# Where sixteen modulation blocks are multiplied: inside the recurrent scan instead of in the readout and the delta merge

## The chip, the cores and the metric

The kernel runs on one core of a Trainium2 chip. The metric is the device time of one execution in microseconds (us), the median of several runs. TensorE multiplies, VectorE (DVE) and ScalarE (ACT) do elementwise work, GpSimd (POOL) a part of the masks, SyncE (SP) issues most DMAs. All data is float32; a large product is computed from pairs of rounded high and low parts.

## The reference, cut to what matters

Three residual layers over 256 tokens of width 1024 (the first two also carry 256 context tokens): a layer with window attention and an mLSTM, an RWKV-7 layer, and a layer with a gated delta rule, an SSD mixer and 32 experts. Each layer is modulated by its condition:

```python
sh_a, sc_a, gt_a, sh_m, sc_m, gt_m = adaln(c, ada_w[layer], ada_b[layer])   # silu(c) @ w + b, split in six
h = rms_norm(x) * (1.0 + sc_a) + sh_a
...
s = s * wt[:, :, None, :] + sa[..., None] * bt[:, :, None, :] + vt[..., None] * kt[:, :, None, :]   # RWKV-7 state
```

`ada_w` of one layer is 1024 x 6144. The kernel cuts it into 12 blocks of 1024 x 512 (2 MB each), and each block is multiplied with the two columns of the condition (latent and context). These products depend on nothing but the condition, so they may stand anywhere ahead of the first use of their values.

## The kernel before

The program is a row of phases. A phase declares its tiles and semaphores, and writes one instruction list for each engine; between two phases all engines meet.

**The ring.** Large weights stream through one ring of three 2 MB slots (class Ring). `plan_ada`, `plan_cols` and `plan_rows` write the order of all its blocks at the start. A phase that takes n blocks calls `ring.issue(sync, n)`, which lets SP issue the loads of these n blocks and of the three after them, each as two DMAs of 1 MB, as soon as the block that held the slot is marked done (`gemm_done`). So up to three blocks of a later phase lie ready when it starts.

**A modulation block** (class Modulate). Eight products of a 128 x 2 weight (the condition) with 128 x 512 of the block; four of them write partitions 0, 32, 64 and 96 of one PSUM bank side by side, and the other four add to them (L746). ACT copies the bank to `mod_row` (L727). Four matmuls with `mod_row` as the weight and the 2-column table `fold` turn the row into columns and add the four parts (L732). At the end DVE adds the bias and writes `g.mods` (L758). The bank is cleared at first, since only two of each 32 partitions are written (L721). In the trace each float32 matmul leaves two records, so a block has 16 matmul records in L746 and 8 in L732.

**The recurrent scan** (`rw_chunks`) does 8 tile steps: four context or latent tiles of 128 tokens forward, then four backward; steps 2, 3, 6 and 7 are latent ones and compute an output too (`read`). A step holds 16 heads, two chunks of 64 tokens and two lanes, all as 64 x 64 matmuls of about 15 to 29 ns each. In order on TensorE: `products`, `first_level`, then levels k = 1 to 5 of a triangular inverse (`level_t`, `level_yx`) with pieces of the next tile's preparation between them (`logits`, `totals` at k = 2, `cumulate` at k = 3), then `solve`, `carry` (products PT on L2217, then G on L2225 and L2229), `read` if latent (L2240 to L2251), `chunk` (L2265, L2278) and `turn_in` of the next tile (L2128). The turn-in waits for ACT's copy of G (L2384) and for DVE's scaled tiles of the next step (L2473 to L2478, semaphore `s_til`).

SP loads k, kk, r of step i once step i-1 has been scaled (`s_til`), and v of step i once G of step i-2 is done.

**The readout** (`rw_readout`) follows the scan: group norm of the output on DVE (L2643 to L2651), then for each of two token tiles seven elementwise steps and the gate (L2656 to L2666), then transposes on TensorE (L2606) and copies on ACT (L2625). TensorE multiplies eight modulation blocks around this. **The delta merge** (`gd_merge`) is built alike (L3486 to L3505 on DVE, transposes L3445, copies L3469) with another eight blocks. `gemm_feat` ("rwout", and "about" in the first layer) and `gemm_rows` ("mixout") are the products after them.

`keep_busy(g, dst, n)` issues n matmuls of 128x128 with 128x256 whose result nobody reads (L482), at the start of many phases.

## Time and profile before

| | us |
|---|---|
| median of 3 runs | 3275.87 (3272.88 to 3277.51) |
| profiled execution, its own time | 3276.72 |
| its span (first to last instruction) | 3274.6 |
| scan, first `products` to the end | 1028.6 to 1529.0 |
| readout | 1529.0 to 1576.3 |
| delta merge | 2121.5 to 2166.4 |

The times in the trace are microseconds from the start of the span. Busy shares of the whole span: TensorE 90%, DVE 41%, ACT 29%, POOL 10%. The shares say little of one stage: the last third of the span is the experts, which stream 400 MB of weights. The stages of the change are in the middle.

### The profile page before, as it was taken

To read this page: it belongs to the slowest core of one execution; us is meant where nothing else is said; L and a number is where in the kernel's file an instruction comes from. 1 tells how busy PE (TensorE), PEld (TensorE's weight loads), DVE (VectorE), ACT (ScalarE), POOL (GpSimd) and SP (SyncE) were. 2 spreads that over 40 slices of the span, in tenths; PEclk is the share of its full clock that TensorE was granted. 3 is DMA by queue.
4 is the path that set the end of the run, shared out by engine and by line. 5 is a ranking of instruction groups with operands and counts; after the bars stand their busy time and mean duration, and the time that the engine had idled before them with its cause. 6 is when DMAs were issued, how large, how long until landed. Compare 5 with 4: busy or idle time off the path is not lost. (4 is left out here: it accounts for less than half of the span.)

```text
span 3274.6 us, 79289 instructions
## 1 busy us (share of the span) xinstructions
PE 2935.4 (90%) x35148; PEld 1967.2 (60%) x35148; DVE 1331.3 (41%) x2021; ACT 948.7 (29%) x1646; POOL 314.5 (10%) x253
## 2 busy tenths in 40 slices
PE   7988899999997788787899988798999998998996
PEld 5865577888575666665799877675333333333332
DVE  3355544333763654555455676464110110110112
ACT  3124433222343333432444563432100100100101
POOL 0021200000321122122000002310000000000001
PEclk9999899999998999999899998988999999999997
DMA  7262412222153100003555432088999999999996
GB/s 267 78 243 78 171 52 103 99 82 103 64 195 114 55 23 23 29 29 109 211 180 181 158 129 81 9 293 306 374 421 421 421 422 421 421 422 421 421 422 265
DMA packets 195063, 681.03 MB, mean 208 GB/s; under 512 B 25616, under 2 KB 40464, under 8 KB 145312
## 3 DMA queue, kind: packets, MB, share of 16 engines
q1 hardware_dynamic: 175328, 651.93, 51.2%
q10 hardware_dynamic: 18336, 21.21, 1.8%
q8 instruction: 203, 3.33, 0.4%
q0 software_dynamic: 1152, 4.19, 0.4%
q14 instruction: 44, 0.36, 0.0%
HBM read 651.86 MB, written 25.43 MB: 207 GB/s over the span
## 5 line engine op out<-in xcount | busy, mean ns | idle before, releaser
L4006 PE MATMUL experts_psum_gu<-ring,experts_x 128*32 128x512 f32 x3840 | 431.4, 597 | 34.6 <-DMA ring<-in_w_gu 34.6
L4128 DVE TENSOR_SCALAR experts_gate<-experts_psum_gu 128x768 f32<-128x768 f32 (+1 forms) x32 | 26.4, 824 | 850.2 <-PE experts_psum_gu L4006 850.2
L4006 PEld LDWEIGHTS experts_psum_gu<-ring,experts_x 128*32 128x32 f32 x3840 | 111.9, 110 | 336.2 <-issue 241.5
L4035 PE MATMUL experts_psum_down<-down_weights,experts_hiddenT 128*32 128x256 f32 x4096 | 231.2, 381 | 15.6 <-DMA down_weights<-in_w_down 12.7
L4035 PEld LDWEIGHTS experts_psum_down<-down_weights,experts_hiddenT 128*32 128x32 f32 x4096 | 127.5, 110 | 128.1 <-DMA down_weights<-in_w_down 32.9
L4072 ACT ACTIVATE experts_sigmoid<-experts_gate 128x768 f32<-128x768 f32 (+1 forms) x32 | 23.6, 737 | 584.9 <-DVE experts_gate L4128 584.9
L991 PE MATMUL mlp_psum_bank<-mlp_x_high,mlp_w_high 128*128 128x512 f32 (+1 forms) x512 | 175.5, 343 | 7.1 <-DVE ring_rounded L315 4.5
L315 DVE TENSOR_TENSOR ring_rounded<-ring,mlp_w_high 128x1024 fp32r<-128x1024 f32 x128 | 156.8, 1225 | 44.4 <-ACT mlp_w_high L310 44.4
L991 PE MATMUL mlp_psum_bank<-xT_rounded,mlp_w_high 128*128 128x512 f32 (+1 forms) x512 | 173.5, 339 | 0.0
L1001 PE MATMUL mlp_psum_bank<-mlp_hidden_high,mlp_w_high 128*128 128x512 f32 (+1 forms) x512 | 172.2, 336 | 1.2 <-ACT mlp_relu L937 1.2
L991 PE MATMUL mlp_psum_bank<-mlp_x_high,ring_rounded 128*128 128x512 f32 (+1 forms) x512 | 173.1, 338 | 0.0
L1001 PE MATMUL mlp_psum_bank<-mlp_hidden_high,ring_rounded 128*128 128x512 f32 (+1 forms) x512 | 172.0, 336 | 0.0
L1001 PE MATMUL mlp_psum_bank<-mlp_hidden_rounded,mlp_w_high 128*128 128x512 f32 (+1 forms) x512 | 172.0, 336 | 0.0
L4006 PE MATMUL experts_psum_gu<-xT,experts_x 128*32 128x512 f32 x1280 | 146.0, 594 | 14.7 <-DMA xT<-in_w_gu 14.7
L2080 POOL TENSOR_TENSOR rwkv_Lo<-rwkv_L,rw_shared 128x512 f32<-128x512 f32 x80 | 101.9, 1285 | 430.6 <-DVE rwkv_L L2512 321.6
L310 ACT CAST mlp_w_high<-ring 128x1024 fp32r<-128x1024 f32 x128 | 133.5, 1043 | 0.0
L991 PEld LDWEIGHTS mlp_psum_bank<-mlp_x_high,mlp_w_high 128*128 128x128 f32 x512 | 97.4, 190 | 20.4 <-issue 5.9
L4006 PEld LDWEIGHTS experts_psum_gu<-xT,experts_x 128*32 128x32 f32 x1280 | 36.7, 110 | 120.6 <-issue 82.4
L4168 POOL DMA_INDIRECT slot_tokens<-moe_y,y_index x8 | 10.2, 1271 | 1018.4 <-POOLq L3949 1016.3
L991 PEld LDWEIGHTS mlp_psum_bank<-mlp_x_high,ring_rounded 128*128 128x128 f32 x512 | 97.8, 191 | 12.2
L1001 PEld LDWEIGHTS mlp_psum_bank<-mlp_hidden_high,mlp_w_high 128*128 128x128 f32 x512 | 97.2, 190 | 11.8 <-ACT mlp_relu L937 1.8
L991 PEld LDWEIGHTS mlp_psum_bank<-xT_rounded,mlp_w_high 128*128 128x128 f32 x512 | 97.0, 189 | 10.5
(793 smaller groups left out, 6052.5 us busy)
## 6 DMA issues: line engine op xcount, KB each, us to landing
ring<-in_w_gu SPq DMA_DIRECT2D x192, 1024.0 KB, 25.9
down_weights<-in_w_down SPq DMA_DIRECT2D x96, 1024.0 KB, 27.2
ring<-in_ada_w SPq DMA_DIRECT2D x72, 1024.0 KB, 10.8
ring<-in_mlp_w SPq DMA_DIRECT2D x64, 1024.0 KB, 7.0
xT<-in_w_gu SPq DMA_DIRECT2D x64, 1024.0 KB, 26.0
ring<-in_w_in SPq DMA_DIRECT2D x24, 1024.0 KB, 6.4
spare_unit<-in_w_down SPq DMA_DIRECT2D x16, 1024.0 KB, 27.1
x<-in_w_down SPq DMA_DIRECT2D x16, 1024.0 KB, 27.3
```

What stands on the lines that cost most here:

```text
L310: self.g.nc.scalar.copy(h, w).then_inc(self.s_high, 1)
L315: self.g.nc.vector.tensor_tensor(low, w, h.bitcast(F32), ALU.subtract).then_inc(self.s_low, 1)
L991: mm = nc.tensor.matmul(banks[:, f % 8, 0:n_tok], w[:, kt, :], x, start=(kt + k == 0), stop=(kt == KT - 1 and k == 2))
L1001: mm = nc.tensor.matmul(banks[:, b, 0:n_tok], w[:, 0, cols], h, start=(f + k == 0), stop=(f == FT - 1 and k == 2))
L2080: v.tensor_tensor(Lo[l][:, :, :], L[l][:, :, :], rep(small(C2_LVL + HALF_LEVELS * d + k), M8), ALU.mult).then_inc(s_lo[l], 1)
L4006: mm = nc.tensor.matmul(pg[32 * j:32 * j + 32, gr, :, :], x, strip(w, j), start=False, stop=(u == U - 1))
L4035: mm = nc.tensor.matmul(pd[32 * c:32 * c + 32, gr, :], hidT[:, a, gr, GROUP * v:GROUP * v + GROUP], w[:, a, C * c:C * c + C], start=(v == ...
L4072: nc.scalar.activation(sg[:, 0:groups, :], gt[:, 0:groups, :], ACT.Sigmoid, scale=SWI_ALPHA).then_inc(s_sg, 1)
L4128: v.tensor_scalar(G, pg[:, 0:groups, 0, :], SWI_LIMIT, None, ALU.min).then_inc(s_gt, 1)
L4168: nc.gpsimd.indirect_dma_start(out=yl[:, n, :], out_offset=None, in_=y_dram[:, :], in_offset=bass.IndirectOffsetOnAxis(ap=yidx[:, t, k:k + ...
```

## The change

1. `rw_chunks` gets a `ScanModulate` with two blocks a tile step, 16 in all: 4 for the RWKV layer's last part and all 12 of the third layer. Products of a step's two blocks go into bank 0 of each lane: those of step 0 after `cumulate(0)` and ahead of the first turn-in, those of step i+1 into the `carry` of step i, between PT and G. ACT copies both rows ahead of its copy of G. The folds of step i stand at k = 2 of step i, ahead of `totals(i + 1)`; ACT keeps their result (two copies of 128x8). TensorE waits for the row copies at the end of `carry`, and for the kept columns ahead of `cumulate`. SP issues the ring's loads behind the v load of each step.
2. The readout has no blocks; it adds the bias of all 16 (`ModulateBias.add`) ahead of its `fetch.wait`. The bias loads are issued behind the others. The square moves from DVE (1 of 1024 a tile) to ACT. `keep_busy` of 6 at the start, of 8 between the two tiles' transposes.
3. The delta merge has no blocks, no `keep_busy` of 4 at the start, and one of 8 between the two tiles' transposes.
4. `keep_busy` at the start goes from `gemm_feat` (5), `mlp` (2 and 4), `ab_merge` (4) and `gemm_rows` (5).

```diff
@@ class ScanModulate (new)
+    def products(self, pe, n, dst):
+        wv = self.ring.take(pe)
+        for kt in range(KT):
+            j = 32 * (kt % 4)
+            if kt == KT // 2:
+                self.ring.wait(pe, self.ring.used - 1, 1)
+            mm = self.g.nc.tensor.matmul(dst[j:j + 2, :], self.g.silu[:, self.dst[n][2] // 2, kt, :], wv[:, kt, :],
+                                         start=(kt < 4), stop=(kt >= 4))
+        self.ring.mark(mm)
+    def copy(self, act, n, src):
+        act.wait_ge(self.ring.gemm_done, self.done0 + n + 1)
+        if n >= self.each:
+            act.wait_ge(self.s_fold, n - self.each + 1)
+        self.g.nc.scalar.copy(self.row[:, n % self.each, :], src).then_inc(self.s_row, 1)
+    def fold(self, pe, n, dst):
+        pe.wait_ge(self.s_row, n + 1)
+        for f in range(4):
+            mm = self.g.nc.tensor.matmul(dst[:, 2 * f:2 * f + 2], self.row[:, n % self.each, f * P:(f + 1) * P], self.g.fold[:, :],
+                                         start=True, stop=True)
+        mm.then_inc(self.s_fold, 1)
+    def keep(self, act, n, src):
+        act.wait_ge(self.s_fold, self.each * (n // self.each + 1))
+        mods, first, _ = self.dst[n]
+        self.g.nc.scalar.copy(mods[:, first:first + 4, :], src.rearrange("p (a b) -> p a b", b=2)).then_inc(self.s_kept, 1)
...
@@ rw_chunks
+        sm = ScanModulate(g, ph, modulate, 2)
+        mod_at = lambda e: banks[e][:, 0, :]
+        fold_at = lambda e: banks[0][:, 3, 16 + 8 * e:24 + 8 * e]
@@ SP, behind the v load of each step, and once at the end
+                    g.ring.issue(sync, sm.each * i)
+                g.ring.issue(sync, sm.each * N)
@@ TensorE, totals(i)
+                    if i:
+                        folds(i - 1)
@@ TensorE, carry(i), between PT and G
+                    if i + 1 < N:
+                        modulate_step(i + 1)
...
+                    if i + 1 < N:
+                        pe.wait_ge(sm.s_row, sm.each * (i + 2))
@@ TensorE, before the loop
                 cumulate(0)
+                pe.wait_ge(s_zero, sm.each)
+                modulate_step(0)
                 take(s_til)
...
@@ rw_readout, TensorE
-                keep_busy(g, ps[:, 0, 0:256], 4)
-                m.step(pe, 0)
-                m.step(pe, 1)
+                keep_busy(g, idle[:, 0:256], 6)
                 gates.wait(pe)
...
-                for k in range(2, m.n - 1):
-                    m.step(pe, k)
                 turned(0)
-                m.step(pe, m.n - 1)
+                keep_busy(g, idle[:, 0:256], 8)
                 turned(1)
@@ rw_readout, DVE
-                    ch.link(nc.vector.tensor_tensor(sq[:, :], yt, yt, ALU.mult))
...
+                m.add(dve)
                 fetch.wait(dve)
@@ gd_merge, TensorE
-                keep_busy(g, ps[:, 0, 0:256], 4)
-                for k in range(m.n - 1):
-                    m.step(pe, k)
                 turned(0)
-                m.step(pe, m.n - 1)
+                keep_busy(g, idle[:, 0:256], 8)
                 turned(1)
@@ gemm_feat and gemm_rows; ab_merge loses its 4, mlp its 2 and 4
-                keep_busy(g, banks[:, 0, 0:256], 5)
@@ the ring's plan
         plan_ada(1, 8, 4)
-        plan_ada(2, 0, 4)
+        plan_ada(2, 0, 12)
...
-        plan_ada(2, 4, 8)
```

## Rows read from the trace of the kernel before

**Rows 1.** Busy time by stage: us, busy (instructions) of five engines, granted clock, DMA share, GB/s

```profile
1028.60:1529.00 500.40, 398.78 (x14312) 335.07 (x14312) 263.42 (x334) 187.74 (x327) 124.56 (x96) 0.97 0.08 27
1143.60:1213.10 69.50, 56.22 (x2000) 47.54 (x2001) 39.27 (x48) 26.35 (x46) 18.46 (x14) 0.98 0.09 27
1529.00:1576.30 47.30, 42.70 (x232) 18.90 (x232) 26.88 (x31) 8.45 (x14) 0.00 (x0) 0.79 1.00 354
2121.50:2166.40 44.90, 39.03 (x232) 19.31 (x232) 26.58 (x27) 15.77 (x23) 0.00 (x0) 0.73 0.92 342
```

**Rows 2.** Timeline of the readout: start, us, engine, line, tiles, count [idle before <- releaser]

```profile
1530.11 1.16 DVE L2643 TENSOR_REDUCE rwread_stats<-rw_y 128x16 f32<-128x1024 f32 x1
...
1541.66 1.23 DVE L2656 TENSOR_TENSOR rw_y<-rw_y,rwread_stats 128x1024 f32<-128x1024 f32 x1 [0.30 <-DMA v_lat<-rw_v]
...
1549.02 1.05 PE L732 MATMUL rwread_psum_mod<-fold,rwread_mod_row 128*128 128x2 f32 x8
...
1550.00 1.90 PE L746 MATMUL rwread_psum_mod_row<-ring,silu 128*2 128x512 f32 x16
...
1556.10 1.29 DVE L2666 TENSOR_TENSOR readout<-rw_y,rwread_psum_gate 128x512 f32<-128x512 f32 x2
...
1574.19 1.07 PE L2606 MATMUL rwread_psum_gate<-const,readout 128*128 128x128 f32 x8
...
1576.40 3.89 PE L482 MATMUL rwout_psum_bank<-const 128*128 128x256 f32 x10 [1.14 <-PEq L2583]
```

**Rows 3.** Timeline of the delta merge

```profile
2121.65 3.27 PE L482 MATMUL gdmerge_psum_turned<-const 128*128 128x256 f32 x8 [2.65 <-PEq L156]
...
2145.88 1.22 DVE L3505 TENSOR_TENSOR mix<-ys,sn 128x1024 f32<-128x1024 f32 x1
...
2152.29 1.23 DVE L3505 TENSOR_TENSOR mix<-ys,sn 128x1024 f32<-128x1024 f32 x1
...
2156.01 3.65 PE L3445 MATMUL gdmerge_psum_turned<-const,mix 128*128 128x128 f32 x16
...
2163.25 1.95 PE L3445 MATMUL gdmerge_psum_turned<-const,mix 128*128 128x128 f32 x16
...
2166.44 2.40 PE L482 MATMUL mixout_psum_bank<-const 128*128 128x256 f32 x10 [1.24 <-PEq L3431]
```

**Rows 4.** DMA queues in scan step 2, 1143.6 to 1213.1: packets, MB, share

```profile
q8 instruction: 16, 0.26, 1.6%
```

**Rows 5.** TensorE's timeline in the carry and read of step 2

```profile
1190.37 1.16 PE L2217 MATMUL rwkv_psum_lane<-rwkv_B,rwkv_A 64*64 64x64 f32 x64
1191.33 1.03 PE L2225 MATMUL rwkv_psum_lane<-rwkv_L,rwkv_B 64*64 64x64 f32 x56
1193.95 0.34 PE L2225 MATMUL rwkv_psum_lane<-rwkv_L,rwkv_B 64*64 64x64 f32 x8 [1.59 <-issue]
...
1197.97 0.34 PE L2240 MATMUL rwkv_psum_lane<-rwkv_mat_BR,rwkv_A 64*64 64x64 f32 x8 [1.93 <-issue]
...
1203.36 0.45 PE L2251 MATMUL rwkv_psum_lane<-x,rwkv_mat_KR 64*64 64x64 f32 x8 [1.56 <-issue]
```

**Rows 6.** Timeline of the carry of step 0

```profile
1078.52 0.62 PE L2229 MATMUL rwkv_psum_lane<-x,rwkv_K 64*64 64x64 f32 x26 [1.64 <-issue]
...
1079.17 1.07 ACT L2384 COPY rwkv_T<-rwkv_psum_lane 128x512 f32<-128x512 f32 x2 [5.26 <-PE rwkv_psum_lane L2229]
...
1080.34 1.07 PE L2128 MATMUL rwkv_psum_lane<-const,rwkv_A 128*128 128x128 f32 x8 [0.31 <-ACT rwkv_T L2384]
```

**Rows 7.** TensorE's timeline at k = 2 of step 0, and ahead of the first turn-in

```profile
1047.32 1.95 PE L2110 MATMUL rwkv_psum_lane<-rw_shared,rwkv_A 128*128 128x2 f32 x16
1049.19 0.69 PE L2179 MATMUL rwkv_psum_lane<-rwkv_T,rwkv_X 64*64 64x64 f32 x32
...
1022.52 1.97 PE L2128 MATMUL rwkv_psum_lane<-const,rwkv_A 128*128 128x128 f32 x8 [5.11 <-DVEq L2480]
```

**Rows 8.** Busy time by stretch around k = 2 of step 0, and at the start of "about"

```profile
1050.40:1053.80 3.40, 3.04 (x118) 2.88 (x112) 0.69 (x1) 2.15 (x4) 0.90 (x1) 0.50 0.02 5
...
404.60:408.70 4.10, 4.10 (x11) 3.29 (x11) 2.98 (x4) 4.10 (x8) 0.00 (x0) 0.50 1.04 387
```

**Rows 9.** SP's timeline in step 2: the loads of k and kk, then of v

```profile
1197.49 0.32 SPq L2059 DMA_DIRECT2D rwkv_loaded<-rw_k  x1
1197.85 0.43 SPq L2059 DMA_DIRECT2D rwkv_loaded<-rw_kk  x1
1203.90 0.32 SPq L2067 DMA_DIRECT2D x<-rw_v  x1
```

More of the change, by code:

```diff
@@ L759, in add, with __init__ @@
                                            ALU.add).then_inc(self.s_end, 1)
+        dve.wait_ge(self.s_end, len(self.parts))
+class ScanModulate:
+    def __init__(self, g, ph, parts, each):
+        self.g, self.ring, self.each = g, g.ring, each
+        self.dst = [(g.mods[layer % 2], 4 * f, layer) for layer, first, n, _ in parts for f in range(first, first + n)]
+        self.row = ph.sb("mod_row", [P, each, 512])
+        self.s_row, self.s_fold, self.s_kept = ph.sem("mod_row"), ph.sem("mod_folded"), ph.sem("mod_kept")
+        self.done0 = self.ring.done
+    def products(self, pe, n, dst):
[22 more added lines that the diff above has]
+        self.g.nc.scalar.copy(mods[:, first:first + 4, :], src.rearrange("p (a b) -> p a b", b=2)).then_inc(self.s_kept, 1)
@@ new lines, with __init__, sync, add @@
+class ModulateBias:
+    def __init__(self, g, ph, parts):
+        self.g, self.parts = g, parts
+        self.bias = ph.sb("mod_bias", [P, 4 * sum(n for _, _, n, _ in parts)])
+        self.s_b, self.s_end = ph.sem("mod_bias"), ph.sem("mod_added")
+    def sync(self, sync):
+        o = 0
+        for _, first, n, bias in self.parts:
+            sync.dma_start(self.bias[:, o:o + 4 * n], bias[:, 4 * first:4 * (first + n)]).then_inc(self.s_b, 16)
+            o += 4 * n
+    def add(self, dve):
+        dve.wait_ge(self.s_b, 16 * len(self.parts))
+        o = 0
+        for layer, first, n, _ in self.parts:
+            dst = self.g.mods[layer % 2][:, 4 * first:4 * (first + n), :]
+            self.g.nc.vector.tensor_tensor(dst, dst, rep(self.bias[:, o:o + 4 * n], 2, 2), ALU.add).then_inc(self.s_end, 1)
+            o += 4 * n
@@ L1980, with rw_chunks @@
 DECAY = math.exp(-0.5)
[L1983 removed]
+def rw_chunks(g, scr, low_w, low_a, w2, a2, ctab, b16, pick, rows, y, coef, tables, s_stored, modulate):
     nc = g.nc
@@ L2091, in _, with modulate_step, folds @@
                 take = Take(pe)
+                def modulate_step(i):
+                    for e in range(sm.each):
+                        sm.products(pe, sm.each * i + e, mod_at(e))
+                def folds(i):
+                    for e in range(sm.each):
+                        sm.fold(pe, sm.each * i + e, fold_at(e))
                 def logits(i, which):
@@ L2292, in _ @@
                 for q in range(nq):
+                    if q == 1:
+                        pe.wait_ge(sm.s_row, sm.each)
                     if q >= 2:
@@ L2313, in _ @@
                             totals(i + 1)
+                        elif k == 2:
+                            folds(i)
+                        if k == 3:
+                            pe.wait_ge(sm.s_kept, sm.each * (i + 1))
                         if nxt and k == 3:
@@ L2395, in _ @@
                 exp_a(0)
+                for e in range(sm.each):
+                    sm.copy(act, e, mod_at(e))
                 turned(0, 0, 4 if lat(0) else 3)
@@ L2417, in _ @@
                                 exp_a(i + 1)
+                        if k == 2:
+                            for e in range(sm.each):
+                                sm.keep(act, sm.each * i + e, fold_at(e))
                         for l in range(2):
@@ L2426, in _ @@
                         copy(lanes(at[i % 2][:, :])[:, :, l, :], banks[l][:, 0, :], s_w[l], s_wc[l])
+                    if nxt:
+                        for e in range(sm.each):
+                            sm.copy(act, sm.each * (i + 1) + e, mod_at(e))
                     for c in range(2):
@@ L2494, in chain @@
                     v.tensor_tensor(new, new, rep(pc[i % 2][:, :, c], CH, 2), ALU.mult).then_inc(s_s, 1)
+                for e in range(sm.each):
+                    v.memset(mod_at(e), 0.0).then_inc(s_zero, 1)
                 mix_k(0)
@@ L2586, in _ @@
                 gates.issue(sync)
-                m.bias_in(sync)
                 fetch.issue(sync)
-                m.ring.issue(sync, m.n)
+                m.sync(sync)
             @block.tensor
             def _(pe):
-                keep_busy(g, ps[:, 0, 0:256], 4)
-                m.step(pe, 0)
-                m.step(pe, 1)
+                keep_busy(g, idle[:, 0:256], 6)
                 gates.wait(pe)
@@ L2617, in _ @@
             def _(act):
-                for k in range(2):
-                    m.copy(act, k)
+                for t in range(2):
+                    act.wait_ge(s_mid, t + 1)
+                    nc.scalar.activation(out[:, t, :], y[:, t, :], ACT.Square).then_inc(s_sq, 1)
                 act.wait_ge(s_var, 1)
@@ L2626, in turned @@
                                        ps[:, 2 * t + j, :].rearrange("p (a b) -> p a b", a=4)).then_inc(s_ev, 1)
-                for k in range(2, m.n - 1):
-                    m.copy(act, k)
-                turned(0)
-                m.copy(act, m.n - 1)
-                turned(1)
+                for t in range(2):
+                    turned(t)
                 act.wait_ge(s_ev, 4)
@@ L3417, in _, with gd_merge @@
                 dve.wait_ge(s_oc, 4)
-def gd_merge(g, p2, og, ys, rows, mix, mixT, fetch, modulate):
+def gd_merge(g, p2, og, ys, rows, mix, mixT, fetch):
     nc = g.nc
@@ L3429, in gd_merge @@
         ps = ph.ps("turned", [P, 4, 512])
-        m = Modulate(g, ph, modulate)
+        idle = ph.ps("idle", [P, 512])
         with nc.Block() as block:
@@ L3461, in _ @@
                             .then_inc(s_sz, 1)
-                for k in range(4):
-                    m.copy(act, k)
                 act.wait_ge(s_ms, 1)
@@ L3470, in turned @@
                                        ps[:, j, :].rearrange("p (a b) -> p a b", a=4)).then_inc(s_ev, 1)
-                for k in range(4, m.n - 1):
-                    m.copy(act, k)
-                turned(0)
-                m.copy(act, m.n - 1)
-                turned(1)
+                for t in range(2):
+                    turned(t)
                 act.wait_ge(s_ev, 8)
@@ L3568, in products @@
                     return mm
-                keep_busy(g, banks[:, 0, 0:256], 5)
                 for k in range(parts):
@@ L4367, in layer1 @@
             rw_chunks(g, scr, low_w, low_a, w2, a2, ctab, b16, pick, {"ka": ka[:, :], "rk": rk[:, :]}, y, coef, tables,
-                      [(s, len(range(i, n_stores, 3))) for i, s in enumerate(s_stored)])
+                      [(s, len(range(i, n_stores, 3))) for i, s in enumerate(s_stored)], modulate)
         both.close()
```

27 lines of the change are left out of this document (12 added, 15 removed).

## The prediction

> **What bounds the kernel now.** I read the page first, then the windows by stage [rows 1]. TensorE is 90% busy over the whole span, but the stages of the change differ. In the scan it works 398.8 of 500.4 us at a granted clock of 0.97, and the DMA engines are nearly idle (share 0.08, 27 GB/s). In the readout and the merge it looks just as busy, but DVE's two token tiles set the end, and the DMA engines are full (1.00 and 0.92; 354 and 342 GB/s). The reader is to see that the change moves TensorE work from stages where something else bounds to one where TensorE leads, and 32 MB of transfers from full engines to idle ones.
>
> Next the timelines. In the readout [rows 2] DVE starts at 1530.11, reaches the value term at 1541.66 with 0.30 us idle (for v_lat), and is done at 1556.10 + 1.29 = 1557.4. But the second tile is turned at 1574.19, since all blocks but one stand ahead of it. The merge [rows 3] has DVE's tiles done at 2147.1 and 2153.5, the turns at 2156.01 and 2163.25.
>
> The scan needs a second look. In the carry of a latent step [rows 5] 64x64 matmuls run back to back: from 1190.37 to 1192.36 (1191.33 + 1.03) are 120 records in 1.99 us, then TensorE stands 1.59 us for nothing but "issue"; from 1193.95 on it works again, and stands 1.93 us ahead of 1197.97; another stall, of 1.56 us, ends 5.4 us later. The queues of that step [rows 4] show 16 instruction transfers, 0.26 MB, so 16 KB each; the step holds 2000 records [rows 1], 125 to a transfer. The spacing of the stalls and the 16 KB agree: I read them as TensorE running ahead of its own instruction stream. A stretch of short matmuls uses 125 records in about 2 us, and a transfer with what surrounds it supplies them in some 3.5 to 4 (1193.95 to 1197.97 is 4.02). The third stall lies behind the loads of k and kk [rows 9]: with them the interval was 5.39 us, 1.4 longer, which I take for contention.
>
> **The change part by part**, against the profiled execution: 3276.72 us (the median of the runs, 3275.87, is 0.85 below it).
>
> *A, readout.* DVE's chain stays: the square (about 1.2 us a tile, as the other 128x1024 operations) goes to ACT, but a semaphore's trip each way and two bias additions come in, so I leave its end at 1557.4. The second turn and the copy took 1576.40 - 1574.19 = 2.2 us [rows 2]; with 0.3 for the handover the output product starts at 1559.9 in place of 1576.4: **-16.5** (-17.5 to -15). What is late next is DVE itself.
>
> *B, merge.* Tile 0 can turn at 2147.3, at half clock 3.65 us [rows 3]; eight `keep_busy` at half clock, another 4, reach 2155.0. That is behind tile 1's end (2153.5), so the filler itself may hold the turn; then 1.95 and the copy, 3.2 together (2163.25 to 2166.44). 2158.2 in place of 2166.4: **-8.2** (-9.5 to -7).
>
> *C, products in seven carries.* A block took 1.90 us for 16 records [rows 2], two 3.8, seven times 26.6. Against it: 32 records last as long as one transfer of instructions. The stream gets one transfer ahead, and the stall in G (1.59 in step 2 [rows 5], 1.64 in step 0 [rows 6]) goes, in latent steps a part of the next too. I take 2.5 us back a step, so 1.3 stays: **+9** (6.5, where only the 32 records count, a quarter of a transfer of 3.7 us a step, to 26.6). ACT's two row copies (0.6 us each, as its 128x512 copies are 1.07 for two [rows 6]) run beside G, whose first 56 records alone take 1.03 [rows 5], about half of it, so TensorE's wait at the end of carry costs nothing; were G's cover gone, it would be 1.2. The turn-in waited 0.31 for ACT's copy of G anyway, so a late copy would show there directly.
>
> *D, folds at k = 2.* 16 records with a 128x128 weight and two columns; `totals` is the same form, 16 in 1.95 us [rows 7]. Seven times 13.6, and a last one under no `totals`. The level waits partly for DVE's and ACT's copies, so I take 1.2 of 1.95, and 0.7 for the last: **+9** (3.8, as 16 records are an eighth of a transfer, to 15.6). Queued behind them are `totals` and the next level's products, for which ACT's and DVE's copies wait.
>
> *E, instruction transfers beside the ring's.* Each step now loads 4.19 MB; at 354 GB/s [rows 1] that is 11.8 us of full engines, behind v, three or four instruction transfers long, so some 25 in all. The only measure is the 1.4 us of [rows 5, 9], beside lighter traffic. Not all are met in short-matmul stretches. I take 0.3 each: **+8** (0 to 20).
>
> *F, clock.* After the 16 two-column matmuls of `totals` the clock stood at 0.50 for 3.4 us (1050.4 to 1053.8) [rows 8], though the scan holds 0.97. Folds double that low stretch at k = 2; seven times 0.35: **+2.5** (0 to 7).
>
> *G, the first tile.* TensorE idled 5.11 us ahead of the first turn-in [rows 7]; 3.8 us of products fit into it, if the three blocks lie ready, and may find it a higher clock: **-1** (-1.7 to +2).
>
> *H, fillers.* `keep_busy` of 5 took 2.40 us at full and 3.89 at half clock [rows 2, 3]. Five phases lose theirs. Where weights are late anyway this is nothing ("about" starts at 0.50 with the DMA engines at 387 GB/s [rows 8]); else it saves 1 to 2 us and gives it back as slower first products. I sum it to **+0.5** (-3 to +4).
>
> Nothing else moves: the ring keeps its order and the experts are shifted as a whole.
>
> **Sum.** -16.5 - 8.2 = -24.7; 9 + 9 + 8 + 2.5 - 1 + 0.5 = +28.0; together +3.3, 3276.7 + 3.3 = 3280.0. Against the median that is +0.13%. Some 0.2% (6.5 us) is what a measurement tells from no change, so it counts as the same.
>
> That TensorE waits for its instructions can be set against the Trainium skill, page "Runtime: NRT & Kernel Launch", section "Instruction fetch mechanics": instructions are refilled in 16 KiB blocks while the present ones execute, and crossing a boundary is "mostly hidden". The 16 KB agree with the row, "hidden" does not (1.6 to 1.9 us of "issue"). By that rule term C would be its full 26.6 and E nothing; it is the first rival. On E, "DMA: Bandwidth & Descriptors", section "Issuing engines are not separate DMA queues", says that transfers started by different engines share the same 16 and interleave; no row here shows an instruction transfer beside full engines. Without it E would stay at its bounds above.
>
> **Rivals.**
> 1. *TensorE's time is all on the path.* The stalls don't come from the stream but return elsewhere, whatever is inserted. C 26.6, D 13.6, F 2.5, E 0, G -1, H 0.5: +42.2 - 24.7 = +17.5, 3294. For it: TensorE is busy 80% of the scan, and the stall follows about every 125 records, which an insertion only shifts. Against it: the added instructions carry few records for their time. 0.2.
> 2. *The loads starve TensorE.* C and D as forecast, but each of the 25 transfers under full engines costs 0.8, E 20, F 4, the rest as in the forecast: +16.8, 3293. For it: one load pair cost 1.4. Against: in step 2 it was on one interval only. 0.15.
> 3. *The scan is bound by the stream of instructions alone* (the other side). Added records cost their share of a transfer and nothing else: C 6.5, D 3.8, E and F 0, G -1.7, H 0.5: +9.1 - 24.7 = -15.6, 3261. It decides if contention is nothing and each stall gives back 2.9 us a step. For it: the stalls of [rows 5, 6] sum to 5.1 us in one carry and read. Against: TensorE also waits for DVE and ACT in the levels, and records are added. 0.27.
> 4. *The moved products do not shorten the merge and readout*, for DVE ends them later (bias, square by semaphore): 3 us each, +9. It is inside the next case's range; I give it no chance of its own.
>
> The forecast, within 6.5 us of before, has 0.38. So faster 0.27, same 0.38, slower 0.20 + 0.15 = 0.35. The range goes from just below the third rival's time to just past the first's: 3260 to 3298; what is left out is C at its full size together with E at its own (over 3300), and a stream-bound scan with merge and readout at their best.
>
> **What the changed profile would show.** The scan 27 to 30 us longer: the latent step of 69.5 us [rows 1] near 73. After PT and the products G without "issue" idle (C right) or with 1.6 us (rival 1). TensorE's "issue" idle larger in the 12 us behind each v load (E). Granted clock at k = 2 low for 5 us or more (F). Readout 31 us, its DVE rows unchanged and the second turn right behind them (A); merge 37 us, and if its second turn waits for nothing, `keep_busy` held it (B). Wrong it would be if stalls are no matter of the stream, if ring blocks come late (loads are issued a step ahead, so against 11.8 us there are some 60), or if lower clocks persist in the phases that lost their fillers.

## The result, and the profile after

The changed kernel takes 3300.52 us (median of 3, 3299.67 to 3308.14) against 3275.87: ratio of the timed runs 1.0089, 95% interval 1.0073 to 1.0106 (the two medians alone give 1.0075). A second set of runs of the same kernel gave 1.0091 (1.0072 to 1.0111). The forecast was 3280.0, "same", with a range of 3260 to 3298: the change makes the kernel 24.7 us slower where 4.1 were forecast, and lands 2.5 us outside the range. The profiled execution has a span of 3298.7 us, 24.1 more than before.

The windows by stage of the changed kernel, beside [rows 1] (scan from TensorE's first product of step 0 to its last matmul, and to the readout; readout; merge; step 2):

```profile
1026.00:1578.40 552.40, 457.08 (x14664) 372.68 (x14664) 262.01 (x332) 197.59 (x357) 123.66 (x96) 0.93 0.24 86
1026.00:1581.80 555.80, 457.08 (x14664) 372.69 (x14665) 263.29 (x334) 197.59 (x357) 123.66 (x96) 0.93 0.24 85
1581.80:1614.60 32.80, 19.50 (x60) 12.59 (x61) 25.25 (x31) 8.73 (x14) 0.00 (x0) 0.76 0.25 85
2157.60:2195.80 38.20, 8.54 (x49) 7.87 (x49) 27.23 (x28) 13.82 (x21) 0.00 (x0) 0.64 0.07 20
1149.60:1231.40 81.80, 66.80 (x2049) 54.34 (x2049) 39.01 (x48) 27.73 (x50) 18.48 (x14) 0.90 0.26 94
```

What to see: the readout and the merge are short, as meant. The scan is 555.8 us in place of 500.4, TensorE busy 457.1 in place of 398.8 (58.3 more), its granted clock 0.93 in place of 0.97; its idle time (552.4 - 457.1 = 95.3) is about what it was (497.0 - 398.8 = 98.2). Step 2 is the sharpest: 81.8 us in place of 69.5, clock 0.90 in place of 0.98.

The start of that step in TensorE's timeline, and below it the window from the first sign of half clock:

```profile
1149.55 3.43 PE L2217 MATMUL rwkv_psum_lane<-xT 64*64 64x64 f32 x203 [0.94 <-DVE xT L2580]
1157.11 1.76 PE L2217 MATMUL rwkv_psum_lane<-xT 64*64 64x64 f32 x53 [4.14 <-issue]
1159.63 1.87 PE L2230 MATMUL rwkv_psum_lane<-rw_shared,rwkv_T 64*64 64x64 f32 x30 [0.76 <-ACT rwkv_mat_KR L2471]
```

```profile
1155.20:1165.40 10.20, 7.53 (x134) 5.95 (x134) 2.29 (x4) 2.46 (x5) 2.49 (x2) 0.50 0.47 174
```

TensorE stands 4.14 us by "issue" (it waits for nothing that the profile shows) in the middle of the products, and from 1155.2 on come 10.2 us at a granted clock of 0.50, in which 30 records take 1.87 us. Before, the same products had this wait:

```profile
1148.54 1.40 PE L2142 MATMUL rwkv_psum_lane<-xT 64*64 64x64 f32 x80 [1.64 <-issue]
```

The queues of 1141 to 1160 show what ran beside the longer wait:

```profile
q1 hardware_dynamic: 2650, 6.22, 88.7%
q8 instruction: 4, 0.07, 1.4%
```

Four instruction transfers in 19 us, and the data transfers take 88.7% of the sixteen engines. Narrow windows of the same view tell when each instruction transfer began. In step 2 of before it was at 1142.4, 1146.0, 1149.7 and 1153.3, one every 3.7 us; here it was at 1148.5, 1154.8, 1159.9 and 1163.5. So the second came 6.3 us behind the first and the third 5.2 behind the second, and with the loads gone the interval is 3.6 again. One of these windows (1154.75 to 1155.00):

```profile
q1 hardware_dynamic: 44, 0.09, 97.2%
q8 instruction: 1, 0.02, 28.1%
```

A transfer itself is no longer than it was (28.1% of sixteen engines in 0.25 us are 1.1 us of one engine; the mean over the scan is 1.06 us before and 1.02 after): it begins late. And TensorE's waits follow these transfers. All 16 "issue" waits of over 1 us in the changed scan end 2.2 to 2.7 us after one began, and so do all 23 of the kernel before: the 4.14 us end at 1157.11, 2.4 behind 1154.8, the 1.64 us of before at 1148.54, 2.6 behind 1146.0. From the first products to the end of the scan no engine's wait ends with the landing of a load, in either trace, so late data are not the cause. The waits of TensorE by line, before and after, in the stretch of the scan (us in total, times, longest), the products' line and then the level's:

```profile
PE rwkv_psum_lane L2142 <- issue: 8.0, 7, 1.7
PE rwkv_psum_lane L2170 <- issue: 16.6, 44, 0.9
```

```profile
PE rwkv_psum_lane L2217 <- issue: 16.8, 7, 4.4
PE rwkv_psum_lane L2245 <- issue: 13.9, 41, 0.7
```

The carry of step 1, where the block products stand (L778):

```profile
1134.81 1.29 PE L2292 MATMUL rwkv_psum_lane<-rwkv_B,rwkv_A 64*64 64x64 f32 x64
1136.03 3.62 PE L778 MATMUL rwkv_psum_lane<-ring,silu 128*2 128x512 f32 x32
1139.57 1.16 PE L2302 MATMUL rwkv_psum_lane<-rwkv_L,rwkv_B 64*64 64x64 f32 x64
1140.56 1.11 PE L2306 MATMUL rwkv_psum_lane<-x,rwkv_K 64*64 64x64 f32 x64
```

No idle time stands in front of the two parts of G; the 1.6 us of [rows 5] and [rows 6] are gone. Over the whole scan, the two lines of G before (L2225, L2229) and all that is left of their waits after:

```profile
PE rwkv_psum_lane L2229 <- issue: 6.3, 4, 1.7
PE rwkv_psum_lane L2225 <- issue: 5.6, 4, 1.6
```

```profile
PE rwkv_psum_lane L2306 <- issue: 1.3, 1, 1.3
```

And k = 2 of step 2, with the folds (L791), and its window:

```profile
1176.63 1.95 PE L791 MATMUL rwkv_psum_lane<-fold,rwkv_mod_row 128*128 128x2 f32 x16
1178.44 2.99 PE L2185 MATMUL rwkv_psum_lane<-rw_shared,rwkv_A 128*128 128x2 f32 x16
1181.36 1.14 PE L2254 MATMUL rwkv_psum_lane<-rwkv_T,rwkv_X 64*64 64x64 f32 x32
```

```profile
1178.40:1185.90 7.50, 7.50 (x178) 7.30 (x177) 0.74 (x1) 2.16 (x7) 1.87 (x1) 0.54 0.01 2
```

The fold takes 1.95 us, `totals` behind it 2.99 in place of 1.95 [rows 7], and the clock is 0.54 in the mean of 7.5 us, so some 6.9 of them at half (worked out from the mean), where [rows 8] had 3.4.

The readout and the merge, as [rows 2] and [rows 3]:

```profile
1581.81 1.22 DVE L2734 TENSOR_REDUCE rwread_stats<-rw_y 128x16 f32<-128x1024 f32 x1 [2.06 <-PEq L156]
...
1593.29 0.36 DVE L820 TENSOR_TENSOR mod<-mod,rwread_mod_bias 128x32 f32<-128x32 f32 x2 [2.90 <-DMA rwread_mod_bias<-in_adab_col]
...
1608.12 1.28 DVE L2760 TENSOR_TENSOR readout<-rw_y,rwread_psum_gate 128x512 f32<-128x512 f32 x2
1609.52 1.09 PE L2702 MATMUL rwread_psum_gate<-const,readout 128*128 128x128 f32 x8 [1.38 <-DVEq L2762]
...
1611.74 0.20 ACT L365 ACTIVATE rwout_token_root<-const 128x4 f32<-128x4 f32 x1 [0.45 <-PEq L2682]
...
1614.62 0.55 PE L626 MATMUL rwout_psum_bank<-rwout_x_high,rwout_w_high 128*128 128x256 f32 x1 [4.00 <-DVE readoutT_rounded L341]
...
2157.63 1.28 ACT L3549 ACT_TABLE_LOAD   x1 [3.85 <-PEq L156]
...
2183.23 3.29 PE L3537 MATMUL gdmerge_psum_turned<-const,mix 128*128 128x128 f32 x16 [28.25 <-DVEq L3589]
...
2186.36 3.62 PE L482 MATMUL gdmerge_psum_idle<-const 128*128 128x256 f32 x16
...
2189.82 1.91 PE L3537 MATMUL gdmerge_psum_turned<-const,mix 128*128 128x128 f32 x16
...
2192.95 0.20 ACT L365 ACTIVATE mixout_token_root<-const 128x4 f32<-128x4 f32 x1 [0.44 <-PEq L3524]
```

DVE's work in the readout lasts from 1581.81 to 1609.4, 27.6 us, and took 27.3 before; a wait of 2.90 us for the bias load has taken the place of the squares that ACT does now. The second turn follows at once.

Where a phase ends is best read from ACT's first instruction of the next one, since TensorE's first was a filler before and is a product now, which waits (4.00 us above). The same places before:

```profile
1576.38 0.20 ACT L365 ACTIVATE rwout_token_root<-const 128x4 f32<-128x4 f32 x1 [0.45 <-PEq L2583]
...
2121.61 1.28 ACT L3460 ACT_TABLE_LOAD   x1 [3.83 <-PEq L156]
...
2166.41 0.20 ACT L365 ACTIVATE mixout_token_root<-const 128x4 f32<-128x4 f32 x1 [0.44 <-PEq L3431]
```

So the readout went from 47.4 to 29.9 us (-17.5), its second turn from 45.2 to 27.7 us behind its start, and the merge from 44.8 to 35.3 (-9.5).

From the first TensorE instruction of one phase to the next one's, in us, the two traces give for the whole kernel (with the reservation just made on the rows behind the readout and the merge):

| | before | after | difference |
|---|---|---|---|
| all ahead of the scan | 998.5 | 997.6 | -0.9 |
| scan (phase) | 530.5 | 584.3 | +53.8 |
| readout | 47.4 | 32.8 | -14.6 |
| output product, up to the delta rule | 466.2 | 464.6 | -1.6 |
| delta rule and merge | 123.9 | 116.5 | -7.4 |
| mixing product and router | 101.3 | 96.5 | -4.8 |
| experts and the end | 1006.9 | 1006.5 | -0.4 |

And the scan by steps, from one first product to the next (to the last matmul for step 7):

| step | 0 | 1 | 2 latent | 3 latent | 4 | 5 | 6 latent | 7 latent |
|---|---|---|---|---|---|---|---|---|
| before | 57.2 | 57.7 | 69.5 | 66.8 | 57.6 | 61.2 | 70.8 | 56.1 |
| after | 62.6 | 61.0 | 81.8 | 77.4 | 62.9 | 63.0 | 85.5 | 58.2 |

The four context steps grew by 15.8 us together, 3.9 each, which is about what the forecast gave every step (28.0 over seven). The latent steps 2, 3 and 6 grew by 37.6, 12.5 each.

### The profile page after: what moved, and what is told of

The parts are those of the page before. It is cut to its first block and busy times, and to the rows that moved or that the text cites. A ratio compares the mean times of both kernels' runs of the same rounds, so it can differ in the third digit from the quotient of the medians.

```text
span 3298.7 us, 79244 instructions
## 1 busy us (share of the span) xinstructions
PE 2928.9 (89%) x35114; PEld 1972.9 (60%) x35114; DVE 1321.2 (40%) x2018; ACT 950.9 (29%) x1664; POOL 313.6 (10%) x253
## 6 DMA issues: line engine op xcount, KB each, us to landing
down_weights<-in_w_down SPq DMA_DIRECT2D x96, 1024.0 KB, 27.7
ring<-in_ada_w SPq DMA_DIRECT2D x72, 1024.0 KB, 11.5
```

## The experiments

Theory 1: the ring's loads keep the DMA engines full, TensorE's instruction transfers come late, and the idle time and what follows it lower the clock; it says where the largest part of the growth comes from. Theory 2, the forecast's first rival: the added products and folds take the time themselves. Three kernels take one part of the change out of the scan each, a fourth restores the fillers.

**Without the loads.** `no_loads` takes the sixteen blocks out of the ring's plan; the products use the three blocks that lie there.

```diff
@@ ScanModulate.products
-        wv = self.ring.take(pe)
+        b = self.ring.used + n % 3
+        self.ring.wait(pe, b, 0)
+        self.ring.wait(pe, b, 1)
+        wv = self.ring.buf[:, b % SLOTS, :].rearrange("p (a b) -> p a b", a=8)
...
-        self.ring.mark(mm)
+        mm.then_inc(self.s_prod, 1)
@@ SP
-                    g.ring.issue(sync, sm.each * i)
-                g.ring.issue(sync, sm.each * N)
@@ the ring's plan
-        plan_ada(1, 8, 4)
-        plan_ada(2, 0, 12)
```

> The changed kernel without the sixteen blocks' loads in the scan: its products multiply whatever the three blocks hold that lie ready when the scan starts, so the modulation values are not the reference's; every product, copy and fold stays. Theory 1 (the loads fill the DMA engines, TensorE's instruction transfers come late in the latent steps' products, and the idle time lowers the clock): the latent steps of 81.8, 77.4 and 85.5 us go to about 73, 70 and 74, 25 to 28 us less in all, 3300 - 26 = 3274. Theory 2 (the added products and folds themselves take the time, wherever it shows): within 5 us of the changed kernel, 3296 to 3301.

Its total (ratio 1.0216, 1.0182 to 1.0250) says nothing, since the modulation values were arbitrary and the experts' phase took 1034 us in place of 973; the scan went from 584.3 to 562.3. `no_loads2` sets the values to zero in the readout:

> The kernel of no_loads once more, with the modulation values of the scan's sixteen blocks set to zero in the readout, so that the experts see ordinary numbers (in no_loads their phase alone took 1034 us in place of 973). By the scan of no_loads (562.3 us from its start to the readout, the changed kernel 584.3, the kernel before 530.5): 22 us less than the changed kernel, about 3279.

Measured: 3276.11 us, ratio 1.0010 (0.9995 to 1.0025), 0.8% under the changed kernel, 26 us. The step starts give 75.0, 70.3 and 73.0 us for steps 2, 3 and 6. That is theory 1's number, and theory 2 as a whole account fails. But products and folds are not free: this kernel, with some 26 us saved in the readout and the merge, is not faster than the one before. The products of step 2 there:

```profile
1144.21 3.43 PE L2217 MATMUL rwkv_psum_lane<-xT 64*64 64x64 f32 x200 [0.94 <-DVE xT L2580]
1149.31 1.04 PE L2217 MATMUL rwkv_psum_lane<-xT 64*64 64x64 f32 x56 [1.67 <-issue]
```

The same stall, at the same place in the instructions, is 1.67 us and not 4.14. The 1.67 that stay are about what the kernel before had there (1.64).

**The loads alone.** Here each block is waited for and marked done, and nothing is multiplied, copied or folded.

```diff
@@ ScanModulate.products
-        wv = self.ring.take(pe)
-        for kt in range(KT):
...
-        self.ring.mark(mm)
+        self.ring.take(pe)
+        self.ring.wait(pe, self.ring.used - 1, 1)
+        pe.sem_inc(self.ring.gemm_done, 1)
+        self.ring.done += 1
```

> The changed kernel with only the loads in the scan: the products, their copies, folds and kept columns are left out (modulation values are missing), TensorE waits for each block and marks it done at the same place. Theory 1: the latent steps keep some 8 to 10 us of their growth, all added TensorE work goes (about 3.5 us a step), the first products stall for 4 us of issue as in the changed kernel: 3300 - 26 = 3274. Theory 2: the loads cost nothing, the scan has its old 500 us: 3300 - 54 = 3247.

Measured: 3278.06 us, ratio 1.0026 (1.0013 to 1.0038). The scan's phase took 556.7, 26 us more than before, with not one matmul added to TensorE's work, and none of its waits in the scan ends with the landing of a block. Theory 1 again. What the changed kernel has above this one, 21 us by the ratios, is products and folds.

**Without the folds.**

```diff
@@ TensorE, totals
-                    if i:
-                        folds(i - 1)
@@ TensorE, levels
-                        elif k == 2:
-                            folds(i)
-                        if k == 3:
-                            pe.wait_ge(sm.s_kept, sm.each * (i + 1))
@@ ACT, level k = 2
-                            for e in range(sm.each):
-                                sm.keep(act, sm.each * i + e, fold_at(e))
```

> The changed kernel without the folds at k = 2 and ACT's kept columns (the modulation values are missing). By the prediction's terms D and F: 9 + 2.5 = 11.5 us less, 3289. If each fold stands in full and draws a longer stretch at half clock behind it: 7 x (1.95 + 1) and more, 20 us less, 3280. If folds are hidden: 4 us less, 3296.

Measured: 3289.37 us, ratio 1.0043 (1.0015 to 1.0071), 15 us under the changed kernel; its scan phase was 560.9, 23 under the changed kernel's and 16 under that of its second trace (`after_again`, below). The forecast was 11.5: the traces say more, the timed runs can't tell 15 from it, with some 11 us on either side. `fold_one` keeps every wait and copy, and drops three of four matmuls:

```diff
@@ ScanModulate.fold
-        for f in range(4):
+        for f in range(1):
@@ ScanModulate.keep
-        self.g.nc.scalar.copy(mods[:, first:first + 4, :], src.rearrange("p (a b) -> p a b", b=2)).then_inc(self.s_kept, 1)
+        self.g.nc.scalar.copy(mods[:, first:first + 4, :], rep(src[:, 0:2], 4)).then_inc(self.s_kept, 1)
```

> The changed kernel with one fold matmul for each block in place of four (its result is copied to all four places, so the modulation values are wrong): 4 records a step at k = 2 in place of 16, the same waits and copies. If the folds' own time and the low clock behind them make the 23 us that no_folds saves in the scan: 15 to 18 us of them go here, scan 567. If the waits around them (row copies, kept columns) make it: less than 6 us go, scan 580.

Measured: ratio 1.0050 (1.0035 to 1.0065), about 13 us under the changed kernel; its scan phase 572.9, 11 under. By the times nearly all that `no_folds` saved, by the trace half of it, or less against the second trace of the changed kernel (4 of 16). What the waits around the folds cost is not settled.

**Without the products.** Loads, row copies, folds and kept columns stay, TensorE's part is that of `loads_only`, and the values are set to zero.

> The changed kernel without the products of the blocks in the scan (TensorE waits for each block and marks it done; loads, row copies, folds and kept columns stay; the modulation values are set to zero in the readout). The prediction's term C says 9 us less than the changed kernel. The runs so far leave 4 to 8 us for it (loads alone 26 more than before in the scan, folds 23, all together 54). If the products stood in full: 25 us less, ratio 1.001.

> The changed kernel itself, beside no_products on the same chip, to see how far the scan's time moves between executions (the scans of no_loads and no_loads2, the same instructions, took 562.3 and 550.5 us from their start to the readout): scan 580 to 590, ratio 1.007 to 1.011.

Measured: `no_products` 1.0081 (1.0049 to 1.0113), `after_again` 1.0091 (1.0072 to 1.0111), scan phases 577.3 and 576.5. The products cost next to nothing: 3 us by the ratios, with an interval of some 12 on either side, none by this pair of traces. The scan of the changed kernel took 584.3 in one trace and 576.5 in the other, those of `no_loads` and `no_loads2`, equal in instructions, 562.3 and 550.5: a difference of under 12 us between two single traces of the scan is worth little.

TensorE in the scan, from its first product to its last matmul, one window for each kernel. In order: before; changed; `no_loads2`; `loads_only`; `no_folds`; `no_products`.

```profile
1028.70:1525.70 497.00, 398.76 (x14312) 335.02 (x14312) 262.13 (x332) 187.74 (x327) 124.56 (x96) 0.97 0.08 27
```

```profile
1020.70:1566.00 545.30, 456.80 (x14664) 373.02 (x14664) 262.47 (x332) 197.45 (x357) 123.50 (x96) 0.93 0.24 87
```

```profile
1022.80:1542.40 519.60, 444.03 (x14664) 362.03 (x14664) 262.32 (x332) 197.51 (x357) 123.45 (x96) 0.95 0.08 27
```

```profile
1024.40:1547.50 523.10, 412.15 (x14312) 346.50 (x14312) 262.30 (x332) 187.45 (x327) 125.44 (x96) 0.93 0.25 90
```

```profile
1022.20:1552.00 529.80, 434.10 (x14536) 348.74 (x14536) 263.83 (x332) 195.55 (x341) 123.61 (x96) 0.94 0.25 90
```

```profile
1025.10:1568.80 543.70, 439.85 (x14440) 376.42 (x14440) 263.56 (x332) 195.91 (x357) 123.47 (x96) 0.91 0.24 86
```

(The second is `after_again`.) These rows part waiting from working. The loads alone: the same 14312 records last 412.2 us in place of 398.8, 13.4 more, and the idle time is 111.0 in place of 98.2, 12.8 more; so half of their 26 us is instructions that come late, and half is the same work at a lower clock. The same loads beside products and folds, `no_loads2` to `after_again`, give the same again: 12.8 us more work and 12.9 more idle time. Products and folds without loads: 45.3 us more work and 22.6 us less idle time (75.6). Products beside the loads, `no_products` to `after_again`: 17 us more work, 15 us less idle time. Seven pairs of blocks at 3.62 us are 25.3, so the rest of the work became 8 us shorter, at a clock of 0.93 in place of 0.91. The give-back that the forecast counted on for the products is there.

**Where the loads stand.** If only the products of latent steps were hurt, the loads could be moved. `late` holds them to level 1, `spread` puts each 1 MB behind an event of its own.

```diff
@@ late, SP
+                    if i:
+                        sync.wait_ge(s_sw, 2 * (i + 1))
                     g.ring.issue(sync, sm.each * i)
@@ spread, SP
+                    if i:
+                        g.ring.issue(sync, sm.each * i, ((s_sw, 2 * (i + 1)), (s_tot, i + 1), (s_cum, 2 * (i + 1)), (s_ea, i + 1)))
+                    else:
+                        g.ring.issue(sync, 0)
@@ spread, Ring.issue, ahead of each of the two loads of a block
+            if gates:
+                sync.wait_ge(*gates.pop(0))
```

> The changed kernel with SP waiting for the w sigmoid of the next tile (at level 1) before the ring loads of a step, so that they run during levels 1 and 2 and not under the products. If only the products and the first level (back to back matmuls without other waits) suffer from late instructions: products of latent steps back to 6 to 7 us, scan 8 to 12 us shorter, 573. If instructions are late wherever the engines are full: the loss moves into the levels, scan within 4 us of 584.

> The changed kernel with each of the four 1 MB loads of a step behind an event of its own (level 1, totals at k = 2, cumulate at k = 3, the exponentials at k = 4). A single 1 MB keeps the DMA engines full for 3 us, shorter than one interval between instruction transfers: if a delay needs a long queue, most of the 22 us go, scan 565. If each byte loaded costs the same: scan 580 to 584.

Measured: `late` 3316.45 us, 1.0124 (1.0098 to 1.0150), scan phase 600.5; `spread` 3297.52, 1.0070 (1.0047 to 1.0092), 581.5. Neither brings the time back. In `late` the products are cured (6.6 and 6.2 us in steps 2 and 3 in place of 10.1 and 10.3), and from the first matmul of level 1 to `totals` it takes 14.0 to 14.8 us in place of about 10.2. TensorE's waits there, the line of `level_t`, and one place:

```profile
PE rwkv_psum_lane L2247 <- issue: 32.7, 44, 3.1
```

```profile
1177.50 0.41 PE L2247 MATMUL rwkv_psum_lane<-rwkv_Y,rwkv_Lo 64*64 64x64 f32 x10 [0.28 <-issue]
1180.79 0.91 PE L2247 MATMUL rwkv_psum_lane<-rwkv_Y,rwkv_Lo 64*64 64x64 f32 x22 [2.88 <-issue]
```

16.6 us of "issue" on that line before, 32.7 here, and the 2.88 us end 2.5 us after an instruction transfer began (at 1178.3, the one before it at 1167.0). The folds behind such a wait run at half clock too: 3.57 us in place of 1.95 in six of the eight steps. So late instructions hurt in each of the three placings tried, and more in the first levels than under the products; spreading the loads in time leaves their price about as it is.

**The fillers.** `fillers` puts the removed `keep_busy` back.

> The changed kernel with the removed keep_busy back at the start of gemm_feat (5), mlp (2 and 4), ab_merge (4) and gemm_rows (5). By the prediction's term H: 0.5 us less, 3300. By the traces of the two kernels, where the phases behind the moved blocks are 1.5 to 2.5 us shorter each without them: 6 to 8 us more, 3307.

Measured: 3298.32 us, ratio 1.0075 (1.0046 to 1.0105), against 1.0089 and 1.0091 without them. The difference can't be told from nothing, on either side. In its trace `ab_merge` up to the RWKV layer's projection is 4.7 us longer than in the changed kernel's, the output product with what follows it 2.1 shorter, and the mixing product 1.5 shorter. (The readout ends at 29.7 us by ACT, as without them.)

**A version for use.** The runs say: a load in the scan costs 26/32 = 0.8 us a MB, folds at k = 2 cost 2 us or more a step, products little, and the readout's second turn is worth most (17.5 us, the merge's 8 to 9.5). `scan2` multiplies just the two blocks ahead of the first turn-in in the scan, the readout keeps six and the merge eight; `scan4` takes two more in the carry of step 0.

```diff
@@ rw_chunks, M = 1 (scan2) or 2 (scan4)
-                    g.ring.issue(sync, sm.each * i)
-                g.ring.issue(sync, sm.each * N)
+                    g.ring.issue(sync, sm.each * min(i, M))
...
-                    if i:
+                    if 0 < i <= M:
                         folds(i - 1)
...
-                    if i + 1 < N:
+                    if i + 1 < M:
                         modulate_step(i + 1)
@@ rw_readout and gd_merge: as before the change, and the readout adds the bias of the scan's blocks
@@ the ring's plan
-        plan_ada(2, 0, 12)
+        plan_ada(2, 0, 4)
...
+        plan_ada(2, 4, 8)
```

> A version for use. Only the two blocks ahead of the first turn-in are multiplied in the scan (TensorE idles 5.1 us there); their folds stand at k = 2 of step 0; the readout keeps six blocks, in the old order around its turns, and the merge its eight; the phases' keep_busy stay removed. By the runs so far (one pair of folds about 2 to 3 us, 4 MB of loads in a context step about 3, the first tile 1.7 less) the scan is 2 to 4 us longer; the readout must load only three blocks, 18 us, and ends near its DVE work, 13 to 16 us earlier; without the fillers 0 to 4 less. Together 10 to 16 us under the kernel before, ratio 0.995 to 0.997. If the readout's blocks still hold the second turn: 4 us under it, 0.999.

> As scan2, with two more blocks in the carry of step 0 (a context step), folded at k = 2 of step 1; the readout keeps four. Scan 6 to 9 us longer than before (steps 0 and 1 of the changed kernel took 8.7 more, the first tile 1.7 to 2.6 less), readout 15 to 17 us shorter: ratio 0.996 to 0.998, 2 to 4 us behind scan2. If the second pair's place makes no difference, equal to scan2.

Measured: `scan2` 3262.52 us, ratio 0.9963 (0.9950 to 0.9976); `scan4` 3263.63, ratio 0.9966 (0.9953 to 0.9979). (One of the six executions of `scan2` took 10648 us, which nothing here explains and the ratio leaves out; the others took 3258 to 3268.) Both beat both kernels, and one can't be told from the other. The second turn of `scan2` stands 31.0 us behind the start of its readout in place of 45.2, its scan phase is 525.0 in place of 530.5, within the scatter. Its turns, with the last of the six blocks between them:

```profile
1546.18 1.07 PE L2703 MATMUL rwread_psum_gate<-const,readout 128*128 128x128 f32 x8
1547.19 1.90 PE L745 MATMUL rwread_psum_mod_row<-ring,silu 128*2 128x512 f32 x16
1549.02 1.95 PE L731 MATMUL rwread_psum_mod<-fold,rwread_mod_row 128*128 128x2 f32 x16
1550.82 1.07 PE L2703 MATMUL rwread_psum_gate<-const,readout 128*128 128x128 f32 x8
1556.85 0.55 PE L626 MATMUL rwout_psum_bank<-rwout_x_high,rwout_w_high 128*128 128x256 f32 x1 [4.96 <-DVE readoutT_rounded L341]
```

## Why the prediction was wrong, by its own steps

*What bounds the kernel.* Right: the scan is where TensorE leads, and it is led by its instruction stream. The stalls by "issue" do come from there: each one of over 1 us ends 2.2 to 2.7 us after an instruction transfer began, and full DMA engines turn one of 1.67 us into one of 4.14 at the same place in the program, with the same instructions. The reading of the third interval in [rows 5] as contention holds too: an instruction transfer began at 1195.5 and the next at 1201.1, 5.5 us later, with the loads of k and kk between them.

*A, readout.* Right in mechanism and near in size: -17.5 against -16.5, at the end of its range. (The table has -14.6, because TensorE's first instruction behind it is now a product that waits 4.00 us, where a filler stood.) DVE ends it, in 27.6 us. The bias wait of 2.90 us was not foreseen, and ate what moving the squares gave.

*B, merge.* -9.5 in this trace and -7.9 in `after_again`, against -8.2 (the table's -7.4 has the same filler in it). `keep_busy` did hold the second turn a little, as said: it lasts 3.6 us, and the turn stands 0.3 us behind DVE's last operation. (The first turn took 3.29 us, where the forecast had 3.65.)

*C, products.* Forecast +9, measured 7 by the traces of `loads_only` and `no_folds` (529.8 - 523.1), 2 by those of `no_products` and `after_again`, 3 by the ratios. The reason was right: the idle time falls by 15 us as 17 us of work come in. The first rival (26.6) is excluded by the traces; the ratios' interval does not exclude half of it.

*D and F, folds and the clock at k = 2.* Forecast 9 + 2.5. Measured 15 by the ratios, with some 11 us on either side, 15.5 and 22.6 by the traces (529.8 to 545.3 and to 552.4). Here nothing was given back: work grew by 23 us from `no_folds` to the changed kernel, of which 15.6 are the folds themselves (eight times 1.95), and idle time stayed at 95.7, 95.3 and 88.5. As far as these traces tell, the step "the level waits partly for DVE's and ACT's copies, so I take 1.2 of 1.95" failed too; and the low stretch behind the folds doubled, from 3.4 to some 6.9 us. Both are sizes, and the timed runs leave the 11.5 possible.

*E, instruction transfers beside the ring's.* This is the main miss, and the step that failed: +8 (0 to 20), 0.3 us for each of 25 transfers. Measured 26 by the traces of `loads_only` and before (523.1 - 497.0), 26 by those of `after_again` and `no_loads2`, and 26 by the ratio of `no_loads2`, with some 7 us on either side. (The timed runs of `loads_only` would make it about 34: they are 8.5 us above before, with some 26 saved in the readout and the merge.) That is one us for each of the 25, above even the second rival's 0.8 and outside the term's own range. The row it rested on said 1.4 us for one transfer beside lighter traffic [rows 5, 9]; the step "not all are met in short-matmul stretches. I take 0.3 each" discounted it by four-fifths with no row for it. `late` and `spread` show no place that forgives a late transfer. And half of the 26 us is not the wait at all but the granted clock behind it, 13.4 us of the same matmuls at a lower clock, which the forecast had only at k = 2.

*G, first tile.* -1.7 (from the phase's start to the first product of step 0: 28.4 us in place of 30.2); forecast -1, with -1.7 as its bound. The block products began at 1017.22 and the first turn-in at 1021.60, so they fit the idle time.

*H, fillers.* Forecast +0.5 (-3 to +4). The traces have -4.3 from `ab_merge` to the RWKV layer's projection, +1.4 behind the readout and +0.2 behind the merge, -3 together; the timed runs have the kernel with its fillers back 2 us faster by the medians and 5 by the ratios. Both are inside the scatter.

*Sum.* Measured terms: -17.5 - 9.5 = -27.0; loads 26, folds 15 to 23, products 2 to 7, first tile -2, the fillers' phases -3: +11 to +24, where 24.1 was measured between the profiled executions. Products, folds and their clock cost 21 us by the ratios of `loads_only` and the changed kernel, where 20.5 were forecast, but there the products' part came out smaller and the folds' larger. So the miss is E. (Two slips in the forecast's working change nothing: the first rival's D is 13.6 where eight folds make 15.6, and the 5.1 us of stalls for the third rival are those of [rows 5] alone.) The second rival, "the loads starve TensorE", is the one that came, with a folds term on top of it; it was given 0.15. Its time, 3293, stood inside the range, its mechanism at the full price did not.

The Trainium skill's page "Runtime: NRT & Kernel Launch", section "Instruction fetch mechanics", has the crossing of a block of instructions "mostly hidden". By that rule the sum would have been all of C and none of E; the runs show the reverse, C nearly nothing and E 26 us. Its page "DMA: Bandwidth & Descriptors", section "Issuing engines are not separate DMA queues", has transfers from different engines share the same 16 and interleave; the transfers that began 6.3 and 5.2 us apart in place of 3.7, and the 4.14 us against 1.67, agree with it for instruction transfers.

What stays open: how much of the folds' price is their time and how much the waits around them (`fold_one` and `no_folds` disagree between trace and times), and what the fillers are worth. Of the clock the runs show that both things lower it: in `loads_only` the matmuls are those of before and the idle time is 12.8 us more (0.93 in place of 0.97), in `no_loads2` the idle time is 22.6 us less and the added matmuls alone are left (0.95). How much each counts in the changed kernel is open. There is one trace of the kernel before, so every difference from it carries that trace's own scatter.

## What to carry to other kernels

As this scan shows, an engine that issues short instructions back to back lives on its own instruction stream, and a weight load that fills the DMA engines is not free beside it, however idle those engines looked (share 0.08); three placings of the loads cost about as much, or more. Price a prefetch there per MB, here 0.8 us. Long instructions of few records were the cheap work to add to this stretch, short ones with tiny outputs the dear one. Before moving work out of a stage, find how much of it must go: here two of the readout's eight blocks brought its second turn 14 of the 17.5 us forward, and the other fourteen blocks together cost more than they gave.

## What the runs showed of the hardware

- TensorE's waits without a visible reason follow the instruction transfers, which carry 16 KB and last about 1.1 us: all 16 of over 1 us in the changed scan, and all 23 before, end 2.2 to 2.7 us after such a transfer began.
- These transfers began 3.7 us apart beside idle DMA engines and 6.3 and 5.2 us apart beside two 2 MB loads and the tile's inputs, with 88.7% of the engines taken. The stall behind the 200th or 203rd record of the same stretch was 1.67 us in the one case and 4.14 us in the other.
- 32 MB of loads with no added matmul cost 26 us of a 497 us stretch, 12.8 as idle time and 13.4 as a granted clock of 0.93 in place of 0.97.
- Sixteen records of two-column matmuls take 1.95 us; sixteen more behind them took 2.99, at a granted clock of 0.54 over 7.5 us.
- Two blocks of eight matmuls each, with 2-column weights and 512 columns (32 records), took 3.62 us and left no stall behind them, where there were 1.6 us before.
- Two traces of the same instructions differed by 8 and by 12 us in the scan alone (584.3 and 576.5; 562.3 and 550.5).
